# A four-layer diffusion trunk on one core: first modulation chunks in pairs, and the queries' norm moved into the exponential

## What is computed

```python
def rmsnorm(x, g):
    y = xf * lax.rsqrt(jnp.mean(xf * xf, axis=-1, keepdims=True) + EPS)
    return (y * g.astype(jnp.float32)).astype(x.dtype)

def ada_mods(cond, w, b):
    mod = (jax.nn.silu(cond) @ w + b)[:, None, :]
    return jnp.split(mod, 6, axis=-1)          # shift, scale, gate, shift, scale, gate

h = modulate(rmsnorm(x, norm_mix[i]), sh1, sc1)
q = rmsnorm(q.reshape(B, L, N_HEADS, HEAD_DIM), q_norm)
k = rmsnorm(k.reshape(B, L, N_KV_HEADS, HEAD_DIM), k_norm)
# latent queries and keys are rotated; scores = q.k / 8, masked; m = max(sink, scores)
# p = exp(s - m); out = sum(p v) / (exp(sink - m) + sum(p))
```

## Time and profile before

| | before |
|---|---|
| median of 3 runs | 2840.65 us |
| the profiled execution | 2844.42 us |
| its span | 2842.6 us |
| mean granted TensorE clock | 0.978 of full speed |
| PE, PE weight load | 2742.6 us (96%), 2595.9 us (91%) |
| DVE, ACT, POOL | 1573.7 us (55%), 1154.9 us (41%), 123.2 us (4%) |
| layer 0's units 2 to 11, first matmul to last | 63.3 to 149.4 us |
| layer 0's first transposes of the attention loop | 167.6 us |
| layer 3's the same two | 2174.1 and 2192.3 us |

### The profile page before, as it was taken

The page is one execution under the profiler, slowest core; times in us unless marked ns, Lnnn a source line. Parts: engine busy times, 40 slices in busy tenths (PEclk is TensorE's granted clock), DMA queues, the critical chain, the costliest instruction groups (busy, mean ns, idle before and its releaser), DMA issues.

```text
span 2842.6 us, 49930 instructions
## 1 busy us (share of the span) xinstructions
PE 2742.6 (96%) x19584; PEld 2595.9 (91%) x19584; DVE 1573.7 (55%) x2665; ACT 1154.9 (41%) x1924; POOL 123.2 (4%) x151
## 2 busy tenths in 40 slices
PE   5989999999998999999899999999998999999999
PEld 4966999999998999999879999999998789999999
DVE  2678366536635664465342665366367946653662
ACT  3357354324425551343232543244244845532440
POOL 1000100000012000000201000000100010000000
PEclk8989899999999999999999999999998999999999
DMA  6123233233321433333201333233221012222222
GB/s 258 60 94 135 83 119 141 107 109 137 143 84 49 145 124 113 119 143 123 84 0 60 126 141 106 110 133 143 73 75 49 2 38 67 74 77 71 71 81 78
DMA packets 62471, 280.48 MB, mean 99 GB/s; under 512 B 7392, under 2 KB 9568, under 8 KB 49632
## 3 DMA queue, kind: packets, MB, share of 16 engines
q1 hardware_dynamic: 62304, 278.07, 27.3%
HBM read 274.88 MB, written 3.16 MB: 98 GB/s over the span
## 4 chain that ended last, share of the span: by engine, by line
PE 91%; DVE 5%; ACT 2%; issue 1%; SPq 1%; DMA 1%; POOL 0%; POOLq 0%; DVEq 0%; ACTq 0%
PE ps L513 77%; PE ps L621 3%; PE ps L716 2%; PE ps L812 2%; PE ps L702 2%; PE ps L687 1%; PE ps L571 1%; DVE prob L1329 1%; PE ps L749 1%; PE ps L579 1%; DMA first_w<-in_ada_w 1%; DVE prob L1345 1%; PE ps L549 1%; DVE h_lo L1186 1%; PE ps L795 0%
## 5 line engine op out<-in xcount | busy, mean ns | idle before, releaser
L513 PE MATMUL ps<-h_hi,w_hi 128*128 128x322 f32 x3552 | 832.5, 316 | 5.6 <-DVE h_lo L1385 1.8
L513 PE MATMUL ps<-h_lo,w_hi 128*128 128x322 f32 x3552 | 823.0, 313 | 0.0
L513 PE MATMUL ps<-h_hi,w_lo 128*128 128x322 f32 x3552 | 817.7, 311 | 0.0
L873 ACT ACTIVATE w_hi<-w_raw 128x1024 fp32r<-128x1024 f32 (+1 forms) x288 | 325.6, 1130 | 1110.4 <-PE ps L513 975.9
L513 PEld LDWEIGHTS ps<-h_hi,w_hi 128*128 128x128 f32 x3552 | 599.0, 190 | 32.1 <-issue 24.7
L513 PEld LDWEIGHTS ps<-h_lo,w_hi 128*128 128x128 f32 x3552 | 605.2, 190 | 0.0
L513 PEld LDWEIGHTS ps<-h_hi,w_lo 128*128 128x128 f32 x3552 | 604.9, 190 | 0.0
L1131 DVE TENSOR_TENSOR w_lo<-w_raw,w_hi 128x1024 fp32r<-128x1024 f32 (+1 forms) x288 | 379.0, 1316 | 118.0 <-ACT w_hi L873 116.2
L1249 DVE SCALAR_TENSOR_TENSOR x<-ps,mods,x 128x321 f32<-128x321 f32 (+5 forms) x264 | 99.8, 434 | 508.1 <-PE ps L513 508.1
L513 PE MATMUL ps<-f_hi,w_hi 128*128 128x322 f32 x1408 | 325.7, 313 | 0.0
L513 PE MATMUL ps<-f_lo,w_hi 128*128 128x322 f32 x1408 | 324.0, 311 | 0.0
(11 more groups left out here) (120 smaller groups left out, 2176.8 us busy)
## 6 DMA issues: line engine op xcount, KB each, us to landing
ada_w<-in_ada_w SPq DMA_DIRECT2D x90, 1024.0 KB, 5.3
w_raw<-in_w_in SPq DMA_DIRECT2D x176, 512.0 KB, 3.2
w_raw<-in_w_out SPq DMA_DIRECT2D x64, 704.0 KB, 4.0
w_raw<-in_w_qkv SPq DMA_DIRECT2D x24, 512.0 KB, 3.2
w_raw<-in_w_o SPq DMA_DIRECT2D x16, 512.0 KB, 3.2
first_w<-in_ada_w SPq DMA_DIRECT2D x6, 1024.0 KB, 15.3
w_raw<-in_w_fnet SPq DMA_DIRECT2D x8, 512.0 KB, 3.3
x<-in_x SPq DMA_DIRECT2D x1, 2576.0 KB, 10.2
```

The source lines that it names most:

```text
L513: mm = pe.matmul(ps[:, 2 * par + hf, 0:NH], w[par][:, kk, :], b[:, hf * NH:(hf + 1) * NH], start=(kk == 0 and n == 0), stop=(kk == k - 1 a ...
L873: act.activation(w_hi[par][:, 0:k, :], w_raw[par][:, 0:k, :], ACT.Copy).then_inc(hi_made, 1)
```

## The change

Two parts. **The start:** the chunks are loaded and multiplied in four pairs (0 and 4, 1 and 5, 2 and 6, 3 and 7), each of which gives shift and scale of two channel tiles. After each pair the row is copied, turned and added, and the gain of two tiles is made. The constants and the weights of units 0 and 1 are loaded ahead of the last six chunks, `conv` behind them. PE runs the two tiles of pair j-1 for both units after the products of pair j, the last two tiles at the end. **The attention:** only the two key tiles are still normed in place. A query tile is rotated un-normed, with tables that carry the query gain; ACT keeps the root of 64 times the mean square with its epsilon (`q_rms`), DVE its reciprocal (`q_scale`) and the negative (`neg_scale`), and the exponential takes `q_scale` as its per-partition scale in place of 1/8. The sink's column is multiplied by `q_rms`. The value tiles are turned after units 5 and 8; the last query's head sum stands inside the first item of the loop, and its rotation on DVE behind the first item's mask.

```diff
-            for c in range(2, 4):
-                load_first(c)
             for dst, src in CONSTS:
                 sp.dma_start(dst[:], t[src]).then_inc(const_in, 16)
-            for c in range(4, 6):
-                load_first(c)
             load_units(0, 2)
-            for c in range(6, FIRST_CHUNKS):
-                load_first(c)
+            for p in range(2, FIRST_CHUNKS):
+                load_first(p)
+            sp.dma_start(conv[:], t["conv"]).then_inc(conv_in, 16)
             sp.wait_ge(ada_mm, FIRST_CHUNKS)
...
-                            pool.tensor_copy(prob[w % 3][:, :, end:end + 1].rearrange("p h c -> p (h c)"),
-                                             sink_col[:, a, head:head + 5:4]).then_inc(sink_put, 1)
+                            pool.wait_ge(q_root, KT * a + tile + 1)
+                            pool.tensor_tensor(prob[w % 3][:, :, end:end + 1].rearrange("p h c -> p (h c)"),
+                                               sink[:, a, head:head + 5:4], q_rms[:, tile, nb, :],
+                                               ALU.mult).then_inc(sink_put, 1)
...
+            def first_unit_tiles(j):
+
+                for kk in (2 * j, 2 * j + 1):
+                    first_tile(0, kk)
+                    first_tile(1, kk)
...
-            for c in range(FIRST_CHUNKS):
-                ada_multiply(0, c, c % 2, chunk_turn(c))
-            ada_turn(0)
+            for j in range(FIRST_PAIRS):
+                for b in range(2):
+                    ada_multiply(j, b, b, 0)
+                ada_turn(j)
+                if j:
+                    first_unit_tiles(j - 1)
             pe.wait_ge(const_in, 16 * len(CONSTS))
+            sum_squares(0, False)
+            for s in range(2):
+                for kk in (KT - 2, KT - 1):
+                    first_tile(s, kk)
+                    if (s, kk) == (1, KT - 2):
+                        turn_back(0)
...
-                        if n >= 3:
+                        if n in (3, 4):
                             turn_heads(layer, n - 3)
...
+                        if n in (5, 8):
+                            v = (n - 5) // 3
...
+                        if w == w0:
+                            sum_heads(layer, 9)
...
+            def query_root(a, tile):
+
+                act.wait_ge(heads_summed, 10 * a + tile + 3)
+                act.activation(q_rms[:, tile, :, :],
+                               ps[:, INV_CTX, SUMS].rearrange("p (b c) -> p b c", c=2), ACT.Sqrt,
+                               bias=eps_wide[:, 0:1], scale=1.0).then_inc(q_root, 1)
...
-                                           bias=st[:, 1:2], scale=HD ** -0.5,
+                                           bias=st[:, 1:2], scale=q_scale[:, tile, nb, hd:hd + 1],
                                            accum_out=st[:, 2:3]).then_inc(exp_made, 1)
...
+            for j in range(FIRST_PAIRS):
+                ada_copy(j, 2 * j + 2)
+                if j == 0:
+                    dve.wait_ge(x_in, 16)
+                else:
+                    gained_low(0, False, range(CT * j - CT, CT * j))
+                first_mods(j)
+                if j == 0:
+                    for u in range(2):
+                        split_lo(u, u, units[u][0])
+            gained_low(0, False, (KT - 2, KT - 1))
...
+                    def query(tile):
+
+                        n = Q0 + tile
+                        dve.wait_ge(q_root, KT * a + tile + 1)
+                        dve.reciprocal(q_scale[:, tile, :, :], q_rms[:, tile, :, :]).then_inc(q_inv, 1)
+                        dve.wait_ge(qkv_out, 12 * a + n + 1)
+                        prompt = qkv[:, n, CTX0:CTX0 + CTX]
+                        dve.tensor_scalar(prompt, prompt, head_gain[:, a, 0:1], None, ALU.mult)
+                        dve.wait_ge(q_inv, KT * a + tile + 1)
+                        dve.tensor_scalar(neg_scale[:, tile, :, :], q_scale[:, tile, :, :], -1.0, None,
+                                          ALU.mult).then_inc(q_scaled, 1)
+                        turn_pairs(qkv[:, n, LAT0:LAT0 + LAT])
...
-                            dve.tensor_scalar(st[:, 1:2], st[:, 0:1], -(HD ** -0.5), neg_sink[:, a, head:head + 1],
+                            if w - w0 < KT and hd == 0:
+                                dve.wait_ge(q_scaled, KT * a + tile + 1)
+                            dve.tensor_scalar(st[:, 1:2], st[:, 0:1], neg_scale[:, tile, nb, hd:hd + 1],
+                                              neg_sink[:, a, head:head + 1],
                                               ALU.mult, ALU.min).then_inc(max_made, 1)
...
                         if w < w0 + 40:
                             masked(w)
+                        if w == w0:
+                            query(KT - 1)
```

More of the change, by code:

```diff
@@ L63 @@
 SQ0 = [sum(2 * KT + (10 if k == "attn" else 0) for k in KINDS[:i]) for i in range(DEPTH)]
-RMS0 = [sum(2 + (10 if k == "attn" else 0) for k in KINDS[:i]) for i in range(DEPTH)]
+RMS0 = [sum(2 + (2 if k == "attn" else 0) for k in KINDS[:i]) for i in range(DEPTH)]
 HFREE0 = [(KT - 1) * sum(k != "pool" for k in KINDS[:i]) for i in range(DEPTH)]
@@ L276, in rms_base @@
         def rms_base(layer, second):
-            return RMS0[layer] + (1 + (10 if KINDS[layer] == "attn" else 0) if second else 0)
+            return RMS0[layer] + (1 + (2 if KINDS[layer] == "attn" else 0) if second else 0)
         def last_update(layer, second, kk):
@@ L482, in _ @@
                         w0 = 40 * a
[L483 removed]
+                        if layer == 0:
+                            pool.wait_ge(const_in, 16 * len(CONSTS))
                         pool.wait_ge(qkv_out, 12 * (a + 1))
@@ L607, in ada_multiply @@
             def ada_multiply(batch, b, par, turn, out=ADA_APART):
-                if batch == 0 and b >= 2:
-                    weights = first_w[b - 2]
-                    pe.wait_ge(first_in[b - 2], 16)
+                if batch < FIRST_PAIRS and batch:
+                    weights = first_w[2 * batch + b - 2]
+                    pe.wait_ge(first_in[2 * batch + b - 2], 16)
                 else:
@@ L836, in _ @@
                         unit(ub + 1, 1, KT, h_tiles, None, ub // 2)
-                    batch = 2 + 2 * layer + half
+                    batch = FIRST_PAIRS + 1 + 2 * layer + half
                     if not last:
@@ L958, in _ @@
             act.activation(cond_act[:], cond_act[:], ACT.Silu).then_inc(cond_made, 1)
-            for kk in range(KT):
+            for kk in range(5):
                 square_tile(0, False, kk)
-                if kk >= KT - 2:
-                    split_hi(kk - KT + 2, kk - KT + 2, units[0][0], 0)
+            for u in range(2):
+                split_hi(u, u, units[u][0], 0)
+            gained(0, False, (0, 1))
+            for kk in range(5, KT):
+                square_tile(0, False, kk)
             act.wait_ge(const_in, 16 * len(CONSTS))
+            gained(0, False, range(2, KT))
             for layer, kind in enumerate(KINDS):
                 u0 = UNIT0[layer]
-                norm(layer, False, KT - 1 if layer and not explicit(layer, False) else 0)
+                norm(layer, False, KT if layer == 0 else 0 if explicit(layer, False) else KT - 1)
                 if kind == "attn":
@@ L986, in _ @@
                         op.then_inc(qkv_out, 1)
-                    root(RMS0[layer] + 10, heads_summed, 10 * (a + 1), 1.0 / HD, 2)
+                    query_root(a, KT - 1)
                     w0 = 40 * a
                     def exps(w):
-                        nb, _ = WORK[w - w0]
+                        nb, tile = WORK[w - w0]
                         lo, hi = KEYS[nb]
@@ L1062, in _ @@
                     norm(layer, True, KT - 1)
+                if layer == 0:
+                    act.wait_ge(conv_in, 16)
                 def up_step(u, par, half_u, pair, v, k_next):
@@ L1168, in gain @@
                 md = mods[layer % 2]
-                dve.wait_ge(ada_done, m + 1 if layer == 0 else 2 * layer + 1 + second)
+                dve.wait_ge(ada_done, FIRST_PAIRS + (1 if layer == 0 else 2 * layer + second))
                 sc = 32 if second else 8
@@ L1172, in gain, with first_mods @@
                                          gains[:, layer, int(second), :, :], ALU.add, ALU.mult).then_inc(gain_made, 1)
-                dve.wait_ge(gain_made, m + 1)
+                dve.wait_ge(gain_made, m + FIRST_PAIRS)
                 if KINDS[layer] == "pool" and not second:
                     own.link(dve.tensor_tensor(pool_gate[:], md[:, 16:16 + KT, :], pool_scale[:], ALU.mult))
+            def first_mods(j):
+                dve.wait_ge(ada_col, j + 1)
+                cols = ADA_APART[1].rearrange("p (n b c) -> p b n c", n=CT, c=2)[:, 0:2, :, :]
+                now = slice(CT * j, CT * j + CT)
+                groups = mods[0][:, 0:2 * KT, :].rearrange("p (g n) c -> p g n c", g=2)[:, :, now, :]
```

(6 more changed lines are left out.)

162 lines of the change are left out of this document (84 added, 78 removed).

## The result

| | before | after |
|---|---|---|
| median | 2841.19 us (5 runs, 2839.8 to 2843.64) | 2824.77 us (5 runs, 2821.62 to 2829.99) |
| ratio of after to before | | 0.9945, 95% interval 0.9931 to 0.996 |
| profiled execution, span | 2844.42, 2842.6 us | 2824.77, 2823.0 us |
| mean granted TensorE clock | 0.978 | 0.985 |
| PE, DVE, ACT busy | 2742.6, 1573.7, 1154.9 us | 2726.4, 1567.2, 1168.4 us |

The change is faster, by 16.4 us between the medians (interval 11 to 20) and by 19.6 between the two profiled spans. What follows asks which of its terms hold. "After" is the changed kernel.

The account below looks back on a forecast made before the run. PE carries 91% of the chain, so only less PE work or waiting wins time. Start 5.8, attention 2 x (2.2 + 5.3) = 15.0, less loop 1.0, gives 19.8 us: 2840.65 - 19.8 = 2821 us, range 2813 to 2832.

Parts of the forecast that it names:

- The start, 5.8: Start of the kernel: tiles run between the chunk products, so unit 2 starts at 57.5 instead of 63.31 us, gaining 5.8.
- that wait shows longer; it is counted: PE's wait ahead of unit 2: six matmuls instead of twelve lie inside the 2.97 us, already included in the sum.
- What was to be late next: Unit 2's weights, loaded after the eighth product: landing at 53.3 us, needed by DVE's split at 55.4 at the earliest.
- The clock rival: In the start the clock never rises from 1.2 GHz: the start loses 7.5 us, total 2834; chance 0.07.
- The products rival: In the start the eight products replace the wait and nothing is gained there: 2827 us; chance 0.11.
- The query units, 2.2 per layer: Query units until unit 11 ends: four groups of turnings of 0.55 us fewer, saving 2.2 us per layer.
- The pause, 5.3 per layer: From unit 11 to the loop: scaled probabilities start at 161.7 instead of 166.93 us, saving 5.3 us per layer.
- about 0.7 in all: DVE per query: reciprocal 0.21, prompt scaling 0.28 and a negation like the reciprocal, together about 0.7 us.
- The exponentials, 0.09 us each, absorbed but for 0.5 per layer: Loop: the second per-partition operand adds 0.09 us per exponential, absorbed by ACT's idle time except 0.5 us per layer.
- The loop, 0.5 per layer: Attention loop: a charge of 0.5 us per layer, for the last eight items, 1.0 us in all.
- DVE's small op (1334) keeps its kind, with a second column for a constant: 0: In the loop, DVE's small operation on the maximum reads a second column instead of a constant at no cost.
- The sum: Whole kernel: 5.8 + 15.0 - 1.0 = 19.8 us saved, profiled span about 2823 us, median 2821 us.

Follow-up runs that it names:

- start_only: The kernel before with only the new start (chunks in pairs, tiles of units 0 and 1 between them) and the old attention code: 2837.42 us, ratio 0.9985.
- after_again: The changed kernel itself, unaltered, run once more on another chip: 2825.24 us, ratio 0.9942.
- exp_const: The changed kernel with the exponential's scale a constant (1/8) again, DVE's small operation keeping its second column: 2825.21 us in one run.
- stat_const: The changed kernel with the factor of DVE's small operation on the maximum a constant (-1/8) again, the exponential keeping its per-partition scale: 2821.98 us in one run.
- one_col: The changed kernel with DVE's small operation multiplying by the neg_scale column alone, the minimum with the sink's column dropped: 2826.9 us in one run.
- low_first: The changed kernel with DVE making the low parts of the previous pair's tiles ahead of the next copy of the row: 2828.0 us in one run.
- adds_late: The changed kernel with the inverse norm turned back six matmuls sooner and GpSimd's last three additions held until two low parts are made: 2820.73 us, one run.

## Why the prediction was right, point by point

- **The start, 5.8: measured 4.5** (`start_only`), 4.8 at unit 2's first matmul and 3.3 behind the clock's fall. The steps were nearly right, some of them by luck. Pair 1's products ended at 27.1, not 28.4; the first low part took 2.3 us and not 1.0; the first tile came at 30.08 for 29.9. Pair 2's products end at 38.5 for 38.1. The groups of 24 tile matmuls take 3.83 and 3.85 us and the 18 take 2.80, where 3.6, 3.5 and 2.7 were put in from a stretch without pauses: together with the rise of the clock, 1 us; with the clock's earlier rise in other executions unit 2 begins at 57.1 to 57.7, and the sum's 57.5 lies among them. The 2.97 us ahead of unit 2 held to 0.01. The step that failed is "that wait shows longer; it is counted": its length was counted, but not that the clock falls behind it, 1.5 us. The text had the clock only as a matter of the tiles.
- **What was to be late next, was not.** Unit 2's weights were there at 54.41, DVE needed them at 57.3.
- **The clock rival** did not come. The matmuls of the first tiles start 0.54 us apart per pair until 36.1 us in after and until 33.9 in after_again, as the earlier trace rows at low clock, and 0.30 apart from then on, through two waits of some 1.5 us each. The case of the Trainium skill's "TensorE: Matmul & The Clock Gate" (HAM oscillation) is one whose DMA waits are longer than the work of a tile, and every tile there ran at half clock. The prediction took it for just this pattern. But here the work is the longer of the two, 3.8 us of tiles between waits of 1.5, so no run tests the page's case. Where the clock did fall, in seven profiles of eight, was behind the wait of 2.09 us, and there the prediction had no rival.
- **The products rival** did not come: they stand in PE's chain at 1.91 us for both, and PE never fell behind the loads.
- **The query units, 2.2 per layer: 2.2.**
- **The pause, 5.3 per layer: 5.9.** The step "about 0.7 in all" for a query's three small operations was too dear: they start 0.12, 0.14 and 0.1 us after one another (146.12 to 146.47), 0.35 in all, twice. Against that, the dearer small operation is in this chain too: with it at 214 ns the pause is 12.05 us, 0.24 shorter.
- **The exponentials, 0.09 us each, absorbed but for 0.5 per layer: right**, by 94, 93 and 91 ns at 513, 385 and 129 columns, and by `exp_const`, whose loops are no shorter. What they cost beside a cheap small operation is nothing in layer 0 and 0.4 us in layer 3, though mostly at the wide items there and not at the 128-column ones that the prediction named. The Trainium skill's "ScalarE: Activation LUTs" (What ACT_TABLE_LOAD costs) gives about 93 ns.
- **The loop, 0.5 per layer: 1.9 to 2.0.** The step that failed is "DVE's small op (1334) keeps its kind, with a second column for a constant: 0". I had priced a column for ACT and not asked the same of DVE. It costs 59 ns, 80 times in each layer, on an engine that PE waits for 12 times in layer 0's loop already; `stat_const` and `one_col` show that it is all of layer 0's 2.0 us and 1.0 of layer 3's 1.9.
- **The sum.** The start came out 1.3 short, the loop 2.9 in all, and the pause gave back 1.2. So 16.8 by these terms for the 19.8 of the forecast, against 16.4 measured. The forecast of the median is right to 3.8 us with each part working as foretold and two prices missed; that the pause made good a part of them is luck. That the two profiled spans differ by 19.6 is partly chance: two stretches of low clock in before's execution are 6.2 us of it, and two in after's take some 3 back. The forecast of the span was right for a reason that it did not give.

## What to carry to other kernels

When an edit puts a column in place of a constant, price it on every engine that gets one, and look first at the engine that the critical one already waits for: 59 ns on DVE cost 2 us in one loop and 1 in the other, 94 ns on ACT at most 0.4. Where DVE's work with two tensors in memory moves onto the critical chain, look at what GpSimd does in the same microseconds, and move that. And once PE has been made dense, weigh each wait that is left twice: its length, and what the granted clock does behind it.

## What the runs showed of the hardware

- DVE's low part of a tile (two tensor inputs) takes 1.0 us alone and 2.29 to 3.65 us beside GpSimd's additions (three of those take 5.2 to 5.5 us then, and 4.9 to 5.0 held back). The Trainium skill's "SBUF — State Buffer" (Who interferes with whom) says that a DVE instruction with two inputs in SBUF contends with a GpSimd instruction that reads SBUF, and that the ports they share are an exclusive lock; the traces agree: in `low_first` the 128x128 instruction of the first low part takes 1.64 us and ends at 26.39, just behind the addition that ran from 24.70 to 26.24. The transfers that ran at the same time did nothing (`adds_late`).
- A second per-partition column costs DVE 59 ns on a 128x1 operation (214 to 273) and ACT 91 to 94 ns on an exponential.
- The clock's rise at the start moves between executions of the same program. Dense work began at 30.08 us in after and at 29.89 in after_again, and the first 24 matmuls took 6.49 and 5.31 us. Runs of one program spread over 8 us (2821.62 to 2829.99), with a mean granted clock of 0.985 in the fastest and 0.979 in the slowest. In one respect the windows, and with them the mean granted clock, can't be trusted: in after they print a clock of 1.00 between 31 and 36 us, while the matmuls stand 0.54 us apart; after_again, with the same spacing, prints 0.50. The spacing is the safer reading.
